# Rotated queries and keys: turned by VectorE in 32x32 squares and moved by DMA, instead of turned by TensorE

## The chip, the cores and the metric

One core of a Trainium2 chip runs the whole program. The metric is the device time of one execution in microseconds, the median of the runs. All times below are microseconds unless they say ns.

## What is computed

Two stacks of two layers each, over 256 tokens of width 1024, in float32. The change touches the first stack alone. Cut to what matters there:

```python
def hybrid_layer(x, ...):
    u = rms_norm(x) @ w_in                       # 1024 x 10240
    qa, ka, va, za, qb, kb, vb, zb, ga, gb = split_cols(u)
    qa, ka = partial_rope(qa), partial_rope(ka)  # 16 heads of 64, first 16 features rotated
    ya = dilated_mixture(qa, ka, va) * silu(za)
    qb, kb = partial_rope(qb), partial_rope(kb)
    ob = diff_attention(qb[0::2], qb[1::2], kb[0::2], kb[1::2], vb, lam)
    yb = rms_norm(ob) * (1 - lam_init) * silu(zb)
    merged = sigmoid(ga) * (ya @ w_proj_a) + sigmoid(gb) * (yb @ w_proj_b)
    return x + merged @ w_out
```

Every attention needs scores q.k for each head. TensorE contracts over partitions, so for the scores the 64 features of a head have to lie on partitions, while the projection leaves tokens on partitions.

## The kernel before

The work is a plan of *pieces*. A weight section of 1024x1024 is two jobs of 512 columns, each of four pieces of 256 rows, so a section is eight pieces. The ten sections of `w_in` come in the order qa, ka, va, za, qb, kb, vb, ga, gb, zb, then the projections pa, pb and out. Numbering the pieces of a layer from 0, qa is 0 to 7, ka 8 to 15, va 16 to 23, za 24 to 31, qb 32 to 39, kb 40 to 47, vb 48 to 55, ga 56 to 63.

SP loads a *unit* (two pieces, 1 MB) into one of four `raw` buffers (line 366), as soon as VectorE has taken the unit that was there (`lo_ready`). ScalarE rounds a piece to `hi` (line 383, ring of 6), VectorE subtracts to get `lo` (line 393, ring of 5, up to three pieces ahead), and TensorE multiplies three times per weight tile: lines 430, 431, 432 (411 and 413, or 420 to 422, where the output is wanted by features). That is twelve 512-column matmuls in a piece.

`plan_one` writes the order by hand: `p.run(jobs, between)` puts the steps of `between[i]` behind piece i of a section. All engines walk the same list of steps, each doing its own part, in order. In the steps around the change:

- `("rope", "qa", tb)`: GpSimd rotates the first 16 features of each head in place, for 128 tokens (lines 1034 to 1039).
- `("turn", "qa", f)`: TensorE transposes four 128x128 blocks into a PSUM bank (`turn_fill`, line 464), and VectorE copies the bank to `qT` or `kT` (line 843). Four of these steps turn a section.
- `("a_scores", h)`, `("b_scores", h)`: TensorE multiplies q and k of heads for attention a (lines 620 and 623, four heads at every fourth step) and for attention b (lines 665 and 666, two at every second). Two heads sit in the two halves of the partitions, and their matmuls run side by side in the array. VectorE takes the maximum with the mask (line 1006).

`buf` are nine buffers of 128x2048: q_tok, k_tok, qT, kT, va, vb, ya, yb, z.

Of the kernel before, what the change touches and what calls it, by code (L numbers as in the profile page):

```python
# [20 lines left out]
ALU = mybir.AluOpType  # L21
# [20 lines left out]
LO_LEAD = 3  # L42
LEVELS = 7
# [205 lines left out]
def plan_one(layer):  # L249

    p = Plan(layer)
    sec = lambda n, i: section(n, "w_in", i * D, 0)
    if layer == 0:
        p.steps += [("turn", "h", 0), ("turn", "h", 1), ("warm", 10)]
    late = lambda name: [("later", name)] if layer == 0 else []
    p.run(sec("qa", 0), [[("turn", "h", 2), ("stat", 0)], [("turn", "h", 3), ("stat", 1), ("rstd",)], ])
    p.run(sec("ka", 1), [[("rope", "qa", 0)], [("rope", "qa", 1)], late("lambda")] + turns("qa"))
    p.run(sec("va", 2), [[("rope", "ka", 0)], [("rope", "ka", 1)], [("half_row",)]] + turns("ka"))
    work = turned_values("a", HEADS)
    p.run(by_features(sec("za", 3)))  # L260
# [12 lines left out]
    p.run(section("out", "w_out", 0, 1), turns("mix", 2) + [[], []] + [ahead(t) for t in turns("h", 0, 2)]  # L273
          + [ahead([("final_row",), ("stat", 0)]) if layer == DEPTH - 1 else []])
    return p


class Core:


    def __init__(self, nc, ctx, ins, plans):
# [32 lines left out]
        self.first_loaded = sem("first_loaded")  # L314

# [38 lines left out]
    def load_unit(self, sp, u):  # L354

        job, n, layer = self.units[u]
        if u >= RAW:
            sp.wait_ge(self.lo_ready, 2 * (u - RAW) + 2)
        slot, k = u % RAW, job.unit
        r0 = (job.row + n * k) * P  # L360
        src = self.ins[job.weight][layer, r0:r0 + k * P, job.col:job.col + job.cols].rearrange("(k p) c -> p k c", p=P)
        dst = self.raw[slot][:, 0:k * job.cols].rearrange("p (k c) -> p k c", k=k)
        if u == 0:
            sp.dma_start(dst[:, 0:k // 2, :], src[:, 0:k // 2, :]).then_inc(self.first_loaded, 16)
            dst, src = dst[:, k // 2:, :], src[:, k // 2:, :]
        sp.dma_start(dst, src).then_inc(self.unit_loaded[slot], 16)

# [168 lines left out]
def block_one(nc, core, s, plans, ins):  # L536
# [5 lines left out]
    target = {"qa": qT, "ka": kT, "qb": qT, "kb": kT}  # L542
    xt_of = {"yb": 0, "mix": 1}
# [16 lines left out]
    parts = [(0, slice(0, P), own), (1, slice(P, 3 * P), both)]  # L560

    @core.program("tensor")
    def _(pe):
        for plan in plans:
            layer, base = plan.layer, plan.base
            turn_at = 0
            for what in plan.all_steps(s):
# [28 lines left out]
                if kind == "turn":  # L596
                    f = what[2]
                    b = (TURN, OUT)[turn_at % 2]
                    turn_at += 1
                    if arg == "h":  # L600
                        turn_input(pe, core, s, b, f)
                        continue
                    core.free(pe, b)
                    if arg in ("qa", "ka", "qb", "kb"):
                        pe.wait_ge(*at("rotated", arg))
                    elif arg == "mix":
# [5 lines left out]
                    core.hold(s, b, "cut" if arg in xt_of else "turn_copied", (arg, f))  # L612
                if kind == "a_scores" and arg % 4 == 0:
                    pe.wait_ge(*at("turn_copied", ("ka", arg // 4)))
                    for two in (arg, arg + 2):
# [42 lines left out]
                if kind == "b_scores" and arg % 2 == 0:  # L658
                    pe.wait_ge(*at("turn_copied", ("kb", arg // 2)))
                    for h in (arg, arg + 1):  # L660
                        for m in range(2):
# [3 lines left out]
                            pe.matmul(B[b][:, 0:P], qT_(qT)[r, h, 0:P], qT_(kT)[r, h, 0:P], start=True, stop=True)  # L665
                            pe.matmul(B[b][:, P:3 * P], qT_(qT)[r, h, P:S], qT_(kT)[r, h, :],  # L666
# [24 lines left out]
    def _(act):  # L691
        for plan in plans:
# [3 lines left out]
            for what in plan.all_steps(s):  # L696
# [41 lines left out]
                if kind == "evac" and arg[:2] in ("zb", "ga", "gb"):  # L738
# [4 lines left out]
                    if arg == "ga0":  # L743
                        act.wait_ge(*at("turned", ("qb", 3)))
                    if arg == "gb0":
                        act.wait_ge(*at("turned", ("kb", 3)))
# [61 lines left out]
    def _(dve):  # L808
        for plan in plans:
            layer, base = plan.layer, plan.base  # L810
            for what in plan.all_steps(s):
# [10 lines left out]
                if kind == "turn":  # L822
# [16 lines left out]
                    else:  # L839
                        dve.wait_ge(*at("turned", (arg, f)))  # L840
                        if arg in ("qb", "kb") and f == 0:
                            dve.wait_ge(*at("a_scored", HEADS - 1))
                        dve.tensor_copy(qT_(target[arg])[:, 2 * f:2 * f + 2, :], bank)\
                           .then_inc(*up("turn_copied", (arg, f)))
                if kind == "evac":
# [4 lines left out]
                    if name in ("qa", "ka", "va", "qb", "kb", "vb"):  # L850
                        if arg == "qb0":
                            dve.wait_ge(*at("turned", ("qa", 3)))
                        if arg == "kb0":
                            dve.wait_ge(*at("turned", ("ka", 3)))
# [64 lines left out]
                if kind == "a_out":  # L919
# [3 lines left out]
                    if arg == 0:  # L923
                        dve.wait_ge(*at("evac", ("za1", "gate", 1)))
                    dve.tensor_tensor(y, B[OUT][:, 0:S], qT_(z)[:, arg, :], ALU.mult).then_inc(*up("ya", arg))
# [32 lines left out]
                if kind == "b_out":  # L958
                    h = arg
                    i = (h % 2) * 2  # L960
                    dve.wait_ge(*at("b_summed", h))
                    dve.tensor_tensor(yb[:, :, h * DV:h * DV + DV],
# [23 lines left out]
    def _(sp):  # L986
        for plan in plans:
            for u in range(len(plan.units)):
                if plan.base // 2 + u >= RAW:
                    core.load_unit(sp, plan.base // 2 + u)  # L990
# [403 lines left out]
def block_two(nc, core, s, plans, ins):  # L1394
# [92 lines left out]
    def _(pe):  # L1487
        for plan in plans:
            layer, base = plan.layer, plan.base
            turn_at = 0  # L1490
            for what in plan.all_steps(s):
# [111 lines left out]
                if kind == "decay_sum":  # L1603

                    core.free(pe, TURN)
                    pe.wait_ge(*at("g"))
# [70 lines left out]
                if kind == "betas":  # L1677

                    core.free(pe, b)
                    pe.wait_ge(*at("brk"))  # L1680
# [122 lines left out]
    def _(act):  # L1803
        for plan in plans:
            layer, base = plan.layer, plan.base
            for what in plan.all_steps(s):
# [41 lines left out]
                if kind == "decay":  # L1848
                    act.wait_ge(*at("evac", "ba0"))
                    act.activation(t.beta, t.ba[:, :, 0:DHEADS], ACT.Tanh, scale=0.5).then_inc(*up("beta_tanh"))  # L1850
                    act.wait_ge(*at("abs"))
# [179 lines left out]
    def _(dve):  # L2031
        for plan in plans:
            layer, base = plan.layer, plan.base
            for what in plan.all_steps(s):
# [44 lines left out]
                if kind == "turn":  # L2079
# [39 lines left out]
                    elif arg == "v":  # L2119
                        dve.wait_ge(*at("turned", (arg, f)))  # L2120
                        dve.wait_ge(*at("beta"))
# [6 lines left out]
                    elif arg == "kd":  # L2128
                        dve.wait_ge(*at("turned", (arg, f)))
                        dve.wait_ge(*at("kds"))  # L2130
# [7 lines left out]
                if kind == "decay":  # L2138
                    y = t.ba[:, :, DHEADS:2 * DHEADS]
                    dve.wait_ge(*at("evac", "ba0"))  # L2140
                    dve.tensor_tensor(y, y, bcast(t.dtb_all[:, layer, :], 1, TB), ALU.add).then_inc(*up("y"))
                    dve.wait_ge(*at("y"))
                    dve.scalar_tensor_tensor(t.abs, y, -1.0, y, ALU.mult, ALU.max).then_inc(*up("abs"))
                    dve.wait_ge(*at("beta_tanh"))
                    dve.tensor_scalar(t.beta, t.beta, 0.5, 0.5, ALU.mult, ALU.add).then_inc(*up("beta"))
                    dve.wait_ge(*at("soft", 1))
                    dve.scalar_tensor_tensor(t.soft, y, 0.0, t.abs, ALU.max, ALU.add).then_inc(*up("softplus"))
                    dve.wait_ge(*at("softplus"))
                    dve.tensor_tensor(t.g, t.soft, bcast(t.nega_all[:, layer, :], 1, TB), ALU.mult).then_inc(*up("g"))
# [13 lines left out]
                if kind == "scales":  # L2163
                    dve.wait_ge(*at("rk"))
                    dve.wait_ge(*at("beta"))
                    dve.wait_ge(*at("ec"))
                    dve.wait_ge(*at("rotated", "sq"))
                    dve.tensor_scalar(t.future, core.upper, -1.0, -NEG, ALU.add, ALU.mult).then_inc(*up("future"))
                    dve.tensor_tensor(t.brk, t.beta, t.rk, ALU.mult).then_inc(*up("brk"))
                    dve.tensor_tensor(t.kds, t.ec[:, 1, :], t.rk[:, 0, :], ALU.mult).then_inc(*up("kds"))  # L2170
                    dve.wait_ge(*at("brk"))
                    dve.scalar_tensor_tensor(t.rs, t.ec[:, 0, :], -1.0, t.brk[:, 1, :], ALU.mult, ALU.mult)\
                       .then_inc(*up("rs"))
# [100 lines left out]
                if kind == "rows":  # L2274

                    dve.wait_ge(*at("rows", arg))
                    dve.wait_ge(*at("future"))
# [57 lines left out]
                if kind == "delta_r":  # L2335
                    dve.wait_ge(*at("from_state", arg))
                    dve.wait_ge(*at("rs"))
# [107 lines left out]
    def _(sp):  # L2445
        for plan in plans:
            for u in range(len(plan.units)):
                core.load_unit(sp, plan.base // 2 + u)
# [80 lines left out]
```

## Time and profile before

| | |
|---|---|
| median of 3 runs | 1710.27 us (1710.21 to 1710.49) |
| profiled execution, first to last instruction | 1709.1 us, TensorE's granted clock 0.999 |
| its own time as a run | not listed; the median of the runs stands 1.2 us above the span |
| TensorE, VectorE, ScalarE, GpSimd busy | 99%, 68%, 56%, 13% of the span |

Busy time counts an instruction from start to end; matmuls overlap each other, so what a matmul costs on TensorE is the distance from its start to the start of the next one. A group of rows "x4" in a timeline is four instructions merged. A float32 matmul that is no transpose appears as two MATMUL records.

### The profile page before, as it was taken

Reading aid. Unit: us, or ns where it says so; the run is one execution under the profiler, and the core shown is the slowest. Engines: PE = TensorE matmul, PEld = TensorE weight load, DVE = VectorE, ACT = ScalarE, POOL = GpSimd, SP = SyncE. Lnnn points to the kernel's source line nnn. Section 1 sums busy time; section 2 is a strip of 40 time slices with the busy share of each in tenths; the row PEclk is TensorE's granted clock in tenths of the full one; section 3 lists DMA queues with packets and bytes.
Section 4 is the critical chain, followed back from the end, with each engine's and each line's share of the span. In section 5 each row is a group of like instructions: output and inputs, shape, how many; then the busy total and the mean of one; then the engine's idle time right before and its main releaser. Section 6 shows DMA issues by size and latency. Waiting matters only on the chain.

```text
span 1709.1 us, 28116 instructions
## 1 busy us (share of the span) xinstructions
PE 1683.8 (99%) x10761; PEld 1378.8 (81%) x10761; DVE 1167.3 (68%) x2160; ACT 959.5 (56%) x1818; POOL 228.2 (13%) x318
## 2 busy tenths in 40 slices
PE   9999999999999999999999999999999999999998
PEld 7887888888878888876787878888876787778887
DVE  6666667766666676678867766656678867676665
ACT  5358475453674754578645455555677645464553
POOL 2202100022030000332202000000332203000000
PEclk9999999999999999999999999999999999999999
DMA  8443544555434345632323455555632333455552
GB/s 309 161 173 125 172 148 149 193 180 194 152 132 164 135 163 173 232 125 100 124 100 110 161 171 182 180 185 174 222 123 100 124 100 125 149 172 195 181 181 85
DMA packets 137120, 270.09 MB, mean 158 GB/s; under 512 B 5535, under 2 KB 8731, under 8 KB 136987
## 3 DMA queue, kind: packets, MB, share of 16 engines
q1 hardware_dynamic: 134928, 265.44, 45.1%
q10 hardware_dynamic: 2059, 2.85, 0.5%
q8 instruction: 87, 1.43, 0.3%
q14 instruction: 46, 0.38, 0.1%
HBM read 267.23 MB, written 1.05 MB: 157 GB/s over the span
## 4 chain that ended last, share of the span: by engine, by line
PE 85%; ACT 5%; DVE 4%; POOL 3%; issue 2%; DMA 0%; DVEq 0%; POOLq 0%; ACTq 0%; SPq 0%
PE bank L430 21%; PE bank L432 20%; PE bank L431 20%; PE bank L411 5%; PE bank L413 3%; PE bank L464 3%; PE bank L422 1%; PE bank L420 1%; PE bank L421 1%; ACT scratch L1963 1%; ACT hi L383 1%; DVE lo L393 1%; PE bank L1751 1%; DVE buf L2115 1%; PE bank L640 1%
## 5 line engine op out<-in xcount | busy, mean ns | idle before, releaser
L430 PE MATMUL bank<-hi,xhl 128*128 128x512 f32 (+1 forms) x1728 | 700.2, 405 | 3.6 <-DVE lo L393 2.1
L432 PE MATMUL bank<-hi,xhl 128*128 128x512 f32 (+1 forms) x1728 | 673.5, 390 | 0.0
L431 PE MATMUL bank<-lo,xhl 128*128 128x512 f32 (+1 forms) x1728 | 671.2, 388 | 0.0
L393 DVE TENSOR_TENSOR lo<-raw,hi 128x1024 fp32r<-128x1024 f32 (+1 forms) x504 | 613.9, 1237 | 49.5 <-PE bank L432 35.5
L383 ACT ACTIVATE hi<-raw 128x1024 fp32r<-128x1024 f32 (+1 forms) x504 | 519.4, 1050 | 213.7 <-PE bank L432 183.0
L430 PEld LDWEIGHTS bank<-hi,xhl 128*128 128x128 f32 x1728 | 324.7, 188 | 79.0 <-issue 14.5
L432 PEld LDWEIGHTS bank<-hi,xhl 128*128 128x128 f32 x1728 | 324.3, 188 | 70.8
L431 PEld LDWEIGHTS bank<-lo,xhl 128*128 128x128 f32 x1728 | 325.5, 188 | 57.2
L411 PE MATMUL bank<-xhl,hi 128*128 128x512 f32 x384 | 136.0, 398 | 0.0
L413 PE MATMUL bank<-xhl,lo 128*128 128x256 f32 x384 | 107.8, 281 | 0.0
L411 PEld LDWEIGHTS bank<-xhl,hi 128*128 128x128 f32 x384 | 72.1, 188 | 17.8
L528 POOL TENSOR_SCALAR small<-small 128x1 f32<-128x1 f32 (+1 forms) x13 | 4.7, 364 | 575.4 <-ACT scratch L521 575.2
L413 PEld LDWEIGHTS bank<-xhl,lo 128*128 128x128 f32 x384 | 72.5, 189 | 0.5
L2115 DVE SCALAR_TENSOR_TENSOR buf<-bank,small,buf 128x255 f32<-128x255 f32 (+1 forms) x144 | 62.8, 477 | 2.5
L464 PE MATMUL bank<-square,buf 128*128 128x128 f32 x408 | 61.0, 273 | 3.2 <-ACT buf L1915 1.6
L464 PEld LDWEIGHTS bank<-square,buf 128*128 128x128 f32 x408 | 48.5, 140 | 17.2 <-issue 6.8
L1034 POOL TENSOR_TENSOR scratch<-buf,rope 128x128 f32<-128x128 f32 (+1 forms) x24 | 24.6, 1025 | 282.6 <-DVE buf L859 239.0
L859 DVE TENSOR_SCALAR buf<-bank,small 128x512 f32<-128x512 f32 x48 | 33.8, 747 | 40.2 <-PE bank L432 40.2
L2243 DVE TENSOR_TENSOR buf<-bank,buf 128x256 f32<-128x256 f32 x48 | 17.0, 417 | 59.4 <-ACT buf L1948 59.4
L420 PE MATMUL bank<-xhl,hi 128*128 128x256 f32 x192 | 54.6, 285 | 0.0
L1006 DVE CUSTOM_DVE_ANT_0 scratch<-bank,masks 128x128 f32<-128x128 f32 (+1 forms) x128 | 38.8, 350 | 22.9 <-PE bank L666 18.0
L422 PE MATMUL bank<-xhl,lo 128*128 128x256 f32 x192 | 54.3, 283 | 0.0
(323 smaller groups left out, 1944.5 us busy)
## 6 DMA issues: line engine op xcount, KB each, us to landing
raw<-in_w_in SPq DMA_DIRECT2D x135, 1024.0 KB, 5.0
raw<-in_w_ff SPq DMA_DIRECT2D x64, 1024.0 KB, 5.3
raw<-in_w_proj_a SPq DMA_DIRECT2D x8, 1024.0 KB, 5.0
raw<-in_w_proj_b SPq DMA_DIRECT2D x8, 1024.0 KB, 5.0
raw<-in_w_out SPq DMA_DIRECT2D x8, 1024.0 KB, 5.2
raw<-in_w_up_sw SPq DMA_DIRECT2D x8, 1024.0 KB, 4.9
raw<-in_w_up_dn SPq DMA_DIRECT2D x8, 1024.0 KB, 4.9
raw<-in_w_o SPq DMA_DIRECT2D x8, 1024.0 KB, 4.8
```

The lines of the kernel that those rows point to most:

```text
L383: act.activation(self.hi[g % HI_RING][:, 0:w], src, ACT.Copy).then_inc(self.hi_ready, 1)
L393: dve.tensor_tensor(self.lo[g % LO_RING][:, 0:w], src, self.hi[g % HI_RING][:, 0:w].bitcast(F32), ALU.subtract).then_inc(self.lo_ready, 1)
L411: pe.matmul(out, hi, self.xhl[job.xt][:, row, :, :].rearrange("p a t -> p (a t)"), start=first, stop=False, skip_group_check=True)
L413: mm = pe.matmul(out[:, 0:S], lo, xh[:, row, :], start=False, stop=last, skip_group_check=True)
L420: pe.matmul(out, hi, xh[:, row, :], start=first, stop=False, skip_group_check=True)
L422: mm = pe.matmul(out, lo, xh[:, row, :], start=False, stop=last, skip_group_check=True)
L430: pe.matmul(out, xh[:, row, t], self.hi[slot % HI_RING][:, w], start=first, stop=False)
L431: pe.matmul(out, xh[:, row, t], self.lo[slot % LO_RING][:, w], start=False, stop=False)
L432: mm = pe.matmul(out, xl[:, row, t], self.hi[slot % HI_RING][:, w], start=False, stop=last)
L464: mm = pe.transpose(bank[:, (j * TB + tb) * P:(j * TB + tb + 1) * P], src[:, tb, c:c + P], core.ident)
L1006: ins = dve.tensor_tensor_reduce(masked[:, to], bank[:, cols], core.masks[:, which, keys], -SCALE, -NEG if negsink is None else negsink, A ...
L2115: ins_ = dve.scalar_tensor_tensor(y, x, w, y, ALU.mult, ALU.add)
```

## The change

The four sections qa, ka, qb, kb are no longer transposed by TensorE. A step `flip` takes the place of four `turn` steps:

- VectorE turns 32x32 squares (`dve.transpose`, two instructions per section, one per 128 tokens), from the rotated section into a buffer that is free then (`flip_from`). It writes 4-byte elements with a step of 16 elements.
- SP waits for that and issues 16 transfers within SBUF, each of 32 partitions by 512 contiguous elements (2 KB), which put the squares where a full transpose has them. They stand in SP's queue between the weight loads. `load_ahead` issues loads up to a fixed number of pieces ahead, so that SP can walk the steps.
- In `qT` and `kT` neighbouring tokens of a feature now lie 16 elements apart. `flipped(buf, f)` is the view that the score matmuls read, for both operands.
- The ropes of qb and kb stand one section earlier, or one or two pieces earlier. Some semaphores of the second block share a name; their order is the same.

```diff
-    p.run(sec("ka", 1), [[("rope", "qa", 0)], [("rope", "qa", 1)], late("lambda")] + turns("qa"))
-    p.run(sec("va", 2), [[("rope", "ka", 0)], [("rope", "ka", 1)], [("half_row",)]] + turns("ka"))
+    p.run(sec("ka", 1), [[("rope", "qa", 0)], [("rope", "qa", 1)], late("lambda"), [], [("flip", "qa")], [], [], []])
+    p.run(sec("va", 2), [[("rope", "ka", 0)], [("rope", "ka", 1)], [("half_row",)], [], [("flip", "ka")], [], [], []])
...
-    p.run(sec("kb", 5), work[8:16])
-    p.run(sec("vb", 6), [work[16] + [("rope", "qb", 0)], work[17] + [("rope", "qb", 1)], work[18] + [("rope", "kb", 0)], [("rope", "kb", 1)]]
-          + turns("qb"))
+    queries = [[("rope", "qb", 0)], [("rope", "qb", 1)], [], [], [], [("flip", "qb")], [], []]
+    p.run(sec("kb", 5), [a + q for a, q in zip(work[8:16], queries)])
+    p.run(sec("vb", 6), [work[16] + [("rope", "kb", 0)], work[17] + [("rope", "kb", 1)], work[18], [],
+                         [("flip", "kb")], [], [], []])
     work = difference(DHEADS)
-    p.run(sec("ga", 8), turns("kb") + work[:4])
+    p.run(sec("ga", 8), [[]] * 4 + work[:4])
...
+    def load_ahead(self, sp, g):
+
+        while self.units_issued < min(len(self.units), (g + LOAD_LEAD) // 2 + 1):
+            self.load_unit(sp, self.units_issued)
+            self.units_issued += 1
...
+    flip_from = {"qa": ya, "ka": yb, "qb": yb, "kb": ya}
+    def flipped(buf, f):
+
+        return buf[:, :, :].rearrange("p a b -> p (a b)").rearrange("p (t f b) -> p f b t", f=KB, b=TB)[:, f]
...
-                            pe.matmul(B[b][:, 0:P], qT_(qT)[r, h // 2, 0:P], qT_(kT)[r, h // 2, 0:P],
+                            pe.matmul(B[b][:, 0:P], flipped(qT, h // 2)[r, 0], flipped(kT, h // 2)[r, 0],
...
-                            pe.matmul(B[b][:, P:3 * P], qT_(qT)[r, h // 2, P:S], qT_(kT)[r, h // 2, :],
+                            pe.matmul(B[b][:, P:3 * P], flipped(qT, h // 2)[r, 1], flipped(kT, h // 2)[r],
...
+                if kind == "flip":
+
+                    dve.wait_ge(*at("rotated", arg))
...
+                    for tb in range(TB):
+                        y = flip_from[arg][:, :, :].rearrange("p a b -> p (a b)")\
+                            .rearrange("p (j a f t) -> p t j f a", j=4, f=KB, t=TB)[:, tb]
+                        ins = dve.transpose(y, source[arg][:, tb, :].rearrange("p (f j a) -> p j f a", f=KB, j=4))
+                    ins.then_inc(*up("flip_turned", arg))
...
+            for what in plan.all_steps(s):
+                kind, arg = what[0], what[1] if len(what) > 1 else None
+                if kind == "piece":
+                    core.load_ahead(sp, plan.base + arg)
+                if kind == "flip":
+                    y = flip_from[arg][:, :, :].rearrange("p a b -> p (a b)").rearrange("p (j x) -> p j x", j=4)
+                    to = target[arg][:, :, :].rearrange("p a b -> p (a b)").rearrange("p (i x) -> p i x", i=4)
+                    sp.wait_ge(*at("flip_turned", arg))
+                    if arg in ("qb", "kb"):
+                        sp.wait_ge(*at("a_scored", HEADS - 1))
+                    if arg != "qa":
+                        sp.wait_ge(*at("flipped", ({"ka": "qa", "qb": "ka", "kb": "qb"}[arg], 3, 3)))
+                    for i in range(4):
+                        for j in range(4):
+                            sp.dma_start(to[QUARTER * j:QUARTER * (j + 1), i, :], y[QUARTER * i:QUARTER * (i + 1), j, :])\
+                              .then_inc(*up("flipped", (arg, i, j), 16))
```

On TensorE, in section ka of layer 0, before:

```order
L432 MATMUL bank<-hi,xhl 128x512
L464 MATMUL bank<-square,buf 128x128 x4
L430 MATMUL bank<-hi,xhl 128x512
L431 MATMUL bank<-lo,xhl 128x512
L432 MATMUL bank<-hi,xhl 128x512
```

and now, at the same place:

```order
L441 MATMUL bank<-hi,xhl 128x512
L439 MATMUL bank<-hi,xhl 128x512
L440 MATMUL bank<-lo,xhl 128x512
L441 MATMUL bank<-hi,xhl 128x512
L439 MATMUL bank<-hi,xhl 128x512
```

The four transposes between the pieces are gone; the big matmuls around them are the same (line 430 is now 439).

On VectorE, in sections ka and va, before (line 859 takes a section's half out of PSUM):

```order
L393 TENSOR_TENSOR lo<-raw,hi 128x1024
L859 TENSOR_SCALAR buf<-bank,small 128x512 x2
L843 COPY buf<-bank 128x512
L393 TENSOR_TENSOR lo<-raw,hi 128x1024
L843 COPY buf<-bank 128x512
L393 TENSOR_TENSOR lo<-raw,hi 128x1024
L843 COPY buf<-bank 128x512
L393 TENSOR_TENSOR lo<-raw,hi 128x1024
L843 COPY buf<-bank 128x512
```

and now:

```order
L402 TENSOR_TENSOR lo<-raw,hi 128x1024
L877 TENSOR_SCALAR buf<-bank,small 128x512 x2
L402 TENSOR_TENSOR lo<-raw,hi 128x1024
L865 STREAM_TRANSPOSE buf<-buf 128x4x8x32 x2
L402 TENSOR_TENSOR lo<-raw,hi 128x1024 x3
L877 TENSOR_SCALAR buf<-bank,small 128x512 x2
```

Four copies, each between two pieces, became two turns behind each other.

On SP, the whole first layer's loads stood in one run:

```order
L1082 DMA narrow<-in_narrow 128x448
L366 DMA raw<-in_w_in 128x4x512 x36
L366 DMA raw<-in_w_proj_a 128x4x512 x4
L366 DMA raw<-in_w_proj_b 128x4x512 x4
```

and now have the transfers between them:

```order
L369 DMA raw<-in_w_in 128x4x512 x8
L1023 DMA buf<-buf 32x512 x16
L369 DMA raw<-in_w_in 128x4x512 x4
L1023 DMA buf<-buf 32x512 x16
L369 DMA raw<-in_w_in 128x4x512 x13
L1023 DMA buf<-buf 32x512 x16
L369 DMA raw<-in_w_in 128x4x512 x3
L1023 DMA buf<-buf 32x512 x16
```

Sixteen small transfers per section moved in front of every later load.

## Rows read from the trace of the kernel before

**Rows 1.** The page: busy time, share of the span, instructions of each engine.

```profile
PE 1683.8 (99%) x10761; PEld 1378.8 (81%) x10761; DVE 1167.3 (68%) x2160; ACT 959.5 (56%) x1818; POOL 228.2 (13%) x318
```

**Rows 2.** The page: the chain that ended last, share by engine.

```profile
PE 85%; ACT 5%; DVE 4%; POOL 3%; issue 2%; DMA 0%; DVEq 0%; POOLq 0%; ACTq 0%; SPq 0%
```

**Rows 3.** The page's groups: busy us, mean ns | idle us before, releaser.

```profile
L430 PE MATMUL bank<-hi,xhl 128*128 128x512 f32 (+1 forms) x1728 | 700.2, 405 | 3.6 <-DVE lo L393 2.1
```

**Rows 4.** Timeline of TensorE, sections with transposes: start, duration, instruction.

```profile
72.29 0.60 PE L464 MATMUL bank<-square,buf 128*128 128x128 f32 x4
72.64 0.48 PE L430 MATMUL bank<-hi,xhl 128*128 128x512 f32 x1
72.96 0.39 PE L431 MATMUL bank<-lo,xhl 128*128 128x512 f32 x1
...
75.48 0.60 PE L464 MATMUL bank<-square,buf 128*128 128x128 f32 x4
75.84 0.48 PE L430 MATMUL bank<-hi,xhl 128*128 128x512 f32 x1
```

**Rows 5.** Timeline of TensorE, twelve big matmuls and nothing between.

```profile
62.04 0.39 PE L430 MATMUL bank<-hi,xhl 128*128 128x512 f32 x1
...
64.76 0.39 PE L430 MATMUL bank<-hi,xhl 128*128 128x512 f32 x1
```

**Rows 6.** Groups of VectorE, shapes apart: the copies of line 843.

```profile
L843 DVE COPY buf<-bank 128x512 f32<-128x512 f32 x32 | 22.1, 690 | 29.1 <-PE bank L464 29.1
```

**Rows 7.** Timeline of TensorE at the first scores of attention a.

```profile
107.44 0.39 PE L432 MATMUL bank<-hi,xhl 128*128 128x512 f32 x1
107.76 0.49 PE L620 MATMUL bank<-buf 64*128 64x128 f32 x4
108.08 0.60 PE L623 MATMUL bank<-buf 64*128 64x256 f32 x4
108.52 0.39 PE L620 MATMUL bank<-buf 64*128 64x128 f32 x4
108.74 0.60 PE L623 MATMUL bank<-buf 64*128 64x256 f32 x4
109.27 0.50 PE L430 MATMUL bank<-hi,xhl 128*128 128x512 f32 x1
```

**Rows 8.** Groups of VectorE, shapes apart; one line of a source view (ns min/median/max).

```profile
L897 DVE TENSOR_TENSOR buf<-buf 128x1024 f32<-128x1024 f32 x4 | 4.9, 1225 | 0.1
L918 DVE RECIPROCAL small<-small 128x2 f32<-128x2 f32 x32 | 5.0, 156 | 0.7 <-ACT scratch L758 0.7
L2162 DVE COPY small<-bank x4: 165/172/175, 805.3 to 1348.0; 128x16 f32<-128x16 f32 x4
```

**Rows 9.** Windows: busy of PE, PEld, DVE, ACT, POOL; clock, DMA share, GB/s.

```profile
34.00:56.00 22.00, 22.00 (x106) 18.13 (x106) 16.77 (x28) 8.38 (x9) 8.69 (x10) 1.00 0.46 155
134.00:166.00 32.00, 32.00 (x187) 24.28 (x186) 21.19 (x60) 25.50 (x69) 7.04 (x10) 1.00 0.39 132
```

**Rows 10.** Timelines of VectorE, SP, ScalarE and TensorE: the load of piece 32.

```profile
71.20 1.22 DVE L393 TENSOR_TENSOR lo<-raw,hi 128x1024 fp32r<-128x1024 f32 x1
...
77.97 0.37 SPq L366 DMA_DIRECT2D raw<-in_w_in  x1
...
95.53 2.94 ACT L383 ACTIVATE hi<-raw 128x1024 fp32r<-128x1024 f32 x3
...
96.27 4.63 DVE L393 TENSOR_TENSOR lo<-raw,hi 128x1024 fp32r<-128x1024 f32 x4
...
104.92 0.40 PE L430 MATMUL bank<-hi,xhl 128*128 128x512 f32 x1
```

**Rows 11.** Loads: SP's issue (ns), KB and us to landing, SP's waits.

```profile
L366 SPq DMA_DIRECT2D raw<-in_w_in x140: 367/368/1147, 2.1 to 1379.0; - x140
...
raw<-in_w_in SPq DMA_DIRECT2D x135, 1024.0 KB, 5.0
...
buf<-in_positions ACTq DMA_DIRECT2D x2, 0.5 KB, 2.1
...
SPq L366 <- DVE lo L393: 1560.1, 247, 13.4
```

More of the change, by code:

```diff
@@ L42 @@
 LO_LEAD = 3
+LOAD_LEAD = 11
 LEVELS = 7
@@ L314, in __init__ @@
         self.first_loaded = sem("first_loaded")
+        self.units_issued = RAW
     def hold(self, s, bank, name, key=0):
@@ L611, in _ @@
                     core.turn_bank[s.stage, arg, f] = b
-                    core.hold(s, b, "cut" if arg in xt_of else "turn_copied", (arg, f))
+                    core.hold(s, b, "cut", (arg, f))
                 if kind == "a_scores" and arg % 4 == 0:
-                    pe.wait_ge(*at("turn_copied", ("ka", arg // 4)))
+                    if arg == 0:
+                        pe.wait_ge(*at("flipped", ("qa", 3, 3)))
+                        pe.wait_ge(*at("flipped", ("ka", 3, 3)))
                     for two in (arg, arg + 2):
@@ L658, in _ @@
                 if kind == "b_scores" and arg % 2 == 0:
-                    pe.wait_ge(*at("turn_copied", ("kb", arg // 2)))
+                    if arg == 0:
+                        pe.wait_ge(*at("flipped", ("qb", 3, 3)))
+                        pe.wait_ge(*at("flipped", ("kb", 3, 3)))
                     for h in (arg, arg + 1):
@@ L664, in _ @@
                             r = slice(HD * m, HD * m + HD)
-                            pe.matmul(B[b][:, 0:P], qT_(qT)[r, h, 0:P], qT_(kT)[r, h, 0:P], start=True, stop=True)
-                            pe.matmul(B[b][:, P:3 * P], qT_(qT)[r, h, P:S], qT_(kT)[r, h, :],
+                            pe.matmul(B[b][:, 0:P], flipped(qT, h)[r, 0], flipped(kT, h)[r, 0], start=True, stop=True)
+                            pe.matmul(B[b][:, P:3 * P], flipped(qT, h)[r, 1], flipped(kT, h)[r],
                                       start=True, stop=True).then_inc(*up("b_scored", (h, m)))
@@ L743, in _ @@
                     if arg == "ga0":
-                        act.wait_ge(*at("turned", ("qb", 3)))
+                        act.wait_ge(*at("flip_turned", "qb"))
                     if arg == "gb0":
-                        act.wait_ge(*at("turned", ("kb", 3)))
+                        act.wait_ge(*at("flip_turned", "kb"))
                     for tb in range(TB):
@@ L838, in _ @@
                         ins.then_inc(*up("cut", (arg, f)))
[L839 to L844, printed above, removed]
+                if kind == "flip":
+                    dve.wait_ge(*at("rotated", arg))
+                    if arg == "qb":
+                        dve.wait_ge(*at("flipped", ("ka", 3, 3)))
+                    if arg == "kb":
+                        dve.wait_ge(*at("cut", ("ya", HEADS // 2 - 1)))
+                    for tb in range(TB):
[3 more added lines that the diff above has]
+                    ins.then_inc(*up("flip_turned", arg))
                 if kind == "evac":
@@ L961, in _ @@
                     dve.wait_ge(*at("b_summed", h))
+                    if h == 0:
+                        dve.wait_ge(*at("flipped", ("qb", 3, 3)))
                     dve.tensor_tensor(yb[:, :, h * DV:h * DV + DV],
@@ L2164, in _ @@
                     dve.wait_ge(*at("rk"))
-                    dve.wait_ge(*at("beta"))
+                    dve.wait_ge(*at("gates", "beta"))
                     dve.wait_ge(*at("ec"))
                     dve.wait_ge(*at("rotated", "sq"))
[L2168 to L2171, printed above, removed]
+                    dve.tensor_scalar(t.future, core.upper, -1.0, -NEG, ALU.add, ALU.mult).then_inc(*up("scales", "future"))
+                    dve.tensor_tensor(t.brk, t.beta, t.rk, ALU.mult).then_inc(*up("scales", "brk"))
+                    dve.tensor_tensor(t.kds, t.ec[:, 1, :], t.rk[:, 0, :], ALU.mult).then_inc(*up("scales", "kds"))
+                    dve.wait_ge(*at("scales", "brk"))
                     dve.scalar_tensor_tensor(t.rs, t.ec[:, 0, :], -1.0, t.brk[:, 1, :], ALU.mult, ALU.mult)\
-                       .then_inc(*up("rs"))
+                       .then_inc(*up("scales", "rs"))
                 if kind == "f_cut":
@@ L2445, in _ @@
     def _(sp):
-        for plan in plans:
-            for u in range(len(plan.units)):
-                core.load_unit(sp, plan.base // 2 + u)
+        for u in range(core.units_issued, len(core.units)):
+            core.load_unit(sp, u)
 def build(nc, ins, out, tally=None):
```

40 lines of the change are left out of this document (16 added, 24 removed).

## The prediction

> **What bounds the kernel now.** I read the busy shares first: TensorE is busy in 99% of a span of 1709.1 us, VectorE in 68%, ScalarE in 56% [rows 1]. The chain that ended last lies on TensorE for 85%, with ScalarE 5% and VectorE 4% [rows 2]. The costliest group, the first of the three multiplications of a weight tile, has 3.6 us of idle time before it over 1728 instructions, most of it on VectorE's lo [rows 3]. So TensorE is the bound and its own instructions are its time: what leaves its stream is gained, what lengthens one is paid, and the other engines matter only when they come late.
>
> **Transposes removed.** Four sections (qa, ka, qb, kb), four groups each, two layers: 32 groups of four 128x128 transposes. The timeline shows two groups [rows 4]: with one in between, the two big matmuls around it would start 0.23 apart; the group starts at 72.29, the next big matmul at 72.64, and the one behind that only at 72.96. Start to start, 72.64 to 75.84 is one piece of twelve big matmuls with one group: 3.20 us. A piece without a group takes 2.72 us, 62.04 to 64.76 [rows 5]. The difference is 0.48 us. Reading only around the group gives the lower value: 72.29 to 72.96 is 0.67, less one matmul of 0.23, is 0.44; the rest is that the following matmuls start 0.230 instead of 0.227 apart, which need not vanish. So 32 groups are worth 14.1 to 15.4 us. I take 0.47 each: **-15.0 us**.
>
> **Copies removed, squares added on VectorE.** 32 copies of 0.69 us leave, and with them 29.1 us in which VectorE waited for the transposes [rows 6]. In come 16 turns of 128x1024 (two a section). The trace has no such instruction. Lower bound: nothing moves 1024 elements on VectorE in less than the 1.23 us of an SBUF to SBUF operation [rows 8]; so 2.4 us a section against 2.8 removed. Upper bound: three times that row, 3.7 us each, 7.4 us a section, because the results are written with a step of 64 bytes. I take 2 us each. The cover is the lo lead: in 34 to 56 us (section ka) VectorE is busy 16.8 of 22 us, in 134 to 166 us 21.2 of 32 [rows 9]. By my values section ka becomes 16.8 - 2.1 + 4.0 = 18.7 of some 20.5 us. Even 7.4 us are 22 us once; the lead absorbs it (the VectorE row at 96.27 is pieces 31 to 34, so 32 is done at 98.6, and TensorE wants it at 104.92 [rows 10], some 6 us). Cost 0. Without that cover it would be the excess over the lead, in each of eight places.
>
> The Trainium skill, "Vector Engine (DVE) Microarchitecture Reference", section 5.2, gives 2.5 ns a column where the destination steps by 24 words; by that each turn would take an estimated 2.6 us. No row here shows it, and the sum stays as it is.
>
> **Sixteen transfers on SP.** They stand in the same queue as the weight loads. Each issue of a load holds SP for 0.368 us, so 16 hold it 5.9 us [rows 11]; SP has idle time for it, 1560 us of waiting for lo. What is late next is the load behind them. Take ka in layer 0: VectorE is through with lo about 72.4 and turns until 76.4; SP issues until 82.3; the load that went out at 77.97 [rows 10] goes out 4.4 us later. One section moves 1 MB, as much as one load, which lands in 5.0 us [rows 11]; behind it the load lands at 82.3 + 5 + 5 = 92.3. ScalarE wants it at 95.53 and TensorE wants the piece at 104.92 [rows 10]. Bounds for the transfers: 5 us at a load's rate, and 16 times the 2.1 us in which the smallest transfer lands, 34 us, if they ran one by one. I take 5, since a load is itself many rows in flight. Cost 0. The consumers are far: qa and ka are turned in the pieces 12 and 20 and first read at 107.76 [rows 7]; kb is turned after piece 52 and first read after piece 60, eight pieces or 22 us later. So the waits on the landed squares cost nothing either. The three waits of SP (turned, the previous section landed, the last a-score) end before or with the turning; only loads queue behind them.
>
> **Ropes and buffers.** The ropes of qb and kb move one section and one or two pieces ahead; GpSimd is busy 228 us of the span [rows 1]. The renamed semaphores of the second block add no wait. Cost 0.
>
> **Scores read with a step.** This is the disputed term. Both operands of every score matmul now step by 16 elements, 64 bytes. Before, a pair of heads takes 0.22 us for its 128-column and 0.44 us for its 256-column matmuls (108.52 to 108.74, 108.08 to 108.52 [rows 7]), 0.66 us. There are 16 pairs a layer, 8 of attention a and 8 of attention b: 32 pairs, 21 us on the bound engine. The trace has no stepped TensorE operand. What it shows: the fp32r stream of the weights takes 512 columns in 0.227 us, 0.44 ns a column [rows 5]; the fp32 scores take 256 columns in 0.44 us for four instructions in two row groups, 0.85 ns a column and pass. So the same port delivers contiguous words twice as fast as the scores ask. Lower bound of the added cost: 0 (a gain is excluded, nothing is shortened). Upper bound: a stepped word costs a VectorE column, 1.20 ns (1.225 us for 1024 [rows 8]): factor 1.4, +8.6 us. A wider one: every column takes twice its present time, +21 us. The only stepped read in the trace is VectorE's copy of 16 columns out of PSUM, 172 ns, against 156 for two unstepped ones [rows 8], which says little but shows no cliff. I take 0, since the port has a factor of two to spare, and keep +21 for the range.
>
> The Trainium skill speaks against this change here: "Advanced Engine Details and Errata", section "SBUF Cachelines", has 16-byte lines of which at least two hits each are needed for full speed, with a penalty when each access meets another line; at 64 bytes every one does. By my rows' rate, the change is then a question of how large the penalty is: up to a factor of two on the port hides in the fp32 rate, beyond it the scores stretch.
>
> **Sum.** -15.0 + 0 + 0 + 0 = -15.0 against the median: the profiled span of 1709.1 us becomes 1694.1, and with the 1.2 us by which the median stands above the span, **1695.3 us**.
>
> **Rivals.**
> *The stepped reads lengthen the scores* (the other side). If a stepped column takes a second time its present slot, +21.1 - 15.0 = +6.1: 1716.4 us; if three times, +42 - 15 = +27: 1737 us. It decides from the point where the score streams take 1.7 times as long (15.0 of 21.1). For it: every word is in another line, and it hits both operands; the weight loads, 128 stepped columns each, may become the longer side. Against it: the factor of two of the port. A smaller form (1.1 to 1.6 times) leaves 2 to 13 us of gain, 1697 to 1708 us. The skill's line rule is this rival's mechanism.
> *The transfers starve the weight ring.* If the 16 run one by one, a section holds the queue 34 us; a load then comes 34 less the 12 us between its arrival and TensorE's need, some 20 us, too late, eight times: beyond 1800 us. With half the overlap, 15 us a section, a few us in all: 1700 us. For it: one queue, 32 descriptors each; against it: a load of 1 MB that lands in 5.0 us has its rows in flight together, and the distance above.
> *VectorE becomes late.* If a turn takes over 5.5 us, section ka needs 14.7 + 11 = 26 us in 20.5 and the lead is spent; about 3 us in each of four places, 1707 us. Against it: four times the nearest row.
> *The change does not do what it says*: TensorE would have to idle where the transposes stood. With 3.6 us of idle time in the group [rows 3] and leads of 6 us that is excluded but for a few tenths.
>
> **Chances.** Forecast (gain 13 to 16 us) 0.46; scores a little longer or some waits (gain over 3.4 us) 0.11; gains and costs cancel 0.06; scores stretched beyond 1.85 times 0.28; loads starved 0.05; VectorE late 0.04, of which half still gains. 0.2% is 3.4 us, about what a measurement of this kernel can tell from no change. Faster 0.58, same 0.06, slower 0.36. The range must reach into the doubled scores: 1692.5 (0.56 us a group) to 1722 (2.3 times); the rest, with tripled scores and starved loads, is some 0.15 to 0.2. The forecast's own range is 1693 to 1698.
>
> **What would show it.** Right: no L464 transposes in these sections; pieces of 2.72 us there; score matmuls of a pair still 0.66 us apart and their durations (272 and 377 ns) unchanged; turns near 2 us; loads still landing within 5 to 12 us; L430's idle time unchanged. Wrong: score matmuls whose starts lie 0.4 us and 0.9 us apart, or longer weight loads between them; idle time of TensorE before L439 released by lo; ScalarE waiting for a DMA. The stepped read is what would make the prediction wrong.

## The result, and the profile after

The change made the kernel slower: 1717.21 us median (1716.99 to 1717.47, 5 runs) against 1710.27 us (1710.09 to 1710.69, 5 runs), ratio 1.004 with a 95% interval of 1.0028 to 1.0051. The forecast was 1695.3 us, so the time lies 22 us away from it, and within a microsecond of the first rival, "a stepped column takes a second time its present slot", 1716.4 us. It lies inside the wide range and on the other side of no change than the one forecast.

The page of the changed kernel, its busy shares and the group of the first big matmul, beside [rows 1, 3]:

```profile
span 1715.3 us, 27940 instructions
PE 1690.1 (99%) x10633; PEld 1380.4 (80%) x10633; DVE 1175.0 (68%) x2144; ACT 959.5 (56%) x1818; POOL 225.8 (13%) x318
L439 PE MATMUL bank<-hi,xhl 128*128 128x512 f32 (+1 forms) x1728 | 696.9, 403 | 3.6 <-DVE lo L402 2.1
```

TensorE has 128 instructions fewer, is busy 6.3 us longer, and has not waited any longer: 25.2 us of the span lie outside its busy time, 25.3 before, and the 3.6 us of idle time of the first group and their releaser are those of before. So the time did not go into a wait. It is in TensorE's own instructions.

The same piece of section ka, after (start, duration, instruction; twelve big matmuls from the first row to the second), and the first scores of attention a, beside [rows 5, 7]:

```profile
49.36 0.39 PE L439 MATMUL bank<-hi,xhl 128*128 128x512 f32 x1
...
52.08 0.39 PE L439 MATMUL bank<-hi,xhl 128*128 128x512 f32 x1
...
103.03 0.39 PE L441 MATMUL bank<-hi,xhl 128*128 128x512 f32 x1
103.34 0.80 PE L634 MATMUL bank<-buf 64*128 64x128 f32 x4
103.96 1.05 PE L637 MATMUL bank<-buf 64*128 64x256 f32 x4
104.82 0.62 PE L634 MATMUL bank<-buf 64*128 64x128 f32 x4
105.26 1.04 PE L637 MATMUL bank<-buf 64*128 64x256 f32 x4
106.24 0.50 PE L439 MATMUL bank<-hi,xhl 128*128 128x512 f32 x1
```

The piece without transposes takes 2.72 us, as forecast. The group of four heads takes 3.21 us from the start of the big matmul ahead of it to that behind it (103.03 to 106.24), where it took 1.83 us (107.44 to 109.27 in [rows 7]): 1.38 us more. The matmuls of 256 columns start 0.86 us before the next group instead of 0.44, and the 128-column ones 0.44 before theirs instead of 0.22: the distances of 0.9 and 0.4 us that the prediction had named as its sign of being wrong. The source views of the two lines say the same for all 64 records of each (ns min/median/max). The 256-column line before:

```profile
L623 PEld LDWEIGHTS bank<-buf x64: 188/188/188, 108.0 to 491.3; 64*128 64x128 f32 x64
L623 PE MATMUL bank<-buf x64: 376/377/378, 108.1 to 491.5; 64*128 64x256 f32 x64
```

and both lines after:

```profile
L634 PEld LDWEIGHTS bank<-buf x64: 288/295/307, 103.3 to 495.0; 64*128 64x128 f32 x64
L634 PE MATMUL bank<-buf x64: 390/390/575, 103.3 to 495.2; 64*128 64x128 f32 x64
...
L637 PEld LDWEIGHTS bank<-buf x64: 289/298/307, 103.8 to 495.4; 64*128 64x128 f32 x64
L637 PE MATMUL bank<-buf x64: 603/603/609, 104.0 to 495.8; 64*128 64x256 f32 x64
```

Each section, from the start of its first big matmul to that of the next section, layer 0, in us (worked out from the starts in the three traces; the last column is the best version, told below):

```
section   before   after   small_rows
ka         23.69   21.76     21.76
va         23.93   21.99     21.99
qb         29.24   32.00     29.23
kb         31.97   34.73     31.97
vb         26.45   24.66     24.66
ga         26.65   25.99     24.59
gb         29.75   32.61     29.76
zb         27.95   29.36     27.96
```

The other sections differ by less than 0.1 us, and layer 1 repeats the table. The gain is there, in ka, va, vb and ga, 7.7 us a layer. The loss is in the four sections that hold scores: qb, kb and gb have two groups each (+2.8), zb one (+1.4), and ga one of its own, which leaves 0.66 of its 2.06 us of gain. Together the five are 11.2 us a layer (eight groups of 1.38 us are 11.0). For both layers: -15.4 + 22.4, some 7 us. The first big matmul of this execution starts 0.6 us earlier than in that of the kernel before, and the span grew by 6.2.

What VectorE, SP and ScalarE did at section va of layer 0, in the timelines:

```profile
69.25 3.81 DVE L865 STREAM_TRANSPOSE buf<-buf 128x1024 f32<-128x1024 f32 x2
...
73.09 10.58 SPq L1023 DMA_DIRECT2D buf<-buf  x16
83.71 1.71 SPq L369 DMA_DIRECT2D raw<-in_w_in  x3
...
91.12 2.94 ACT L392 ACTIVATE hi<-raw 128x1024 fp32r<-128x1024 f32 x3
```

And over the program, the turns and the issues of the transfers in the source views:

```profile
L865 DVE STREAM_TRANSPOSE buf<-buf x16: 1937/1978/2018, 47.3 to 524.9; 128x1024 f32<-128x1024 f32 x16
...
L1023 SPq DMA_DIRECT2D buf<-buf x128: 507/591/1457, 51.1 to 537.2; - x128
```

The list of DMA issues gives the median from issue to landing in its last column:

```profile
buf<-buf SPq DMA_DIRECT2D x128, 64.0 KB, 2.0
```

A turn took 1.98 us. An issue of a transfer took 0.59 us in the median, not a load's 0.368; with the gaps between them the sixteen held SP for 10.6 us here instead of the forecast 5.9, and three loads queued up behind. The transfers landed 2.0 us after their issue (median), longer than one issue takes, so they overlapped. The loads had enough lead: ScalarE split the same pieces at 91.12, 9.4 us before section qb began at 100.50, the same lead as before the change (95.53 for a start at 104.92 [rows 10]). TensorE did not wait.

### The profile page after: what moved, and what is told of

Its sections match the earlier page's. It is cut to its first block, busy times and chain, and to the rows that moved or that the text cites. A ratio compares the mean times of both kernels' runs of the same rounds, so it can differ in the third digit from the quotient of the medians.

```text
span 1715.3 us, 27940 instructions
## 1 busy us (share of the span) xinstructions
PE 1690.1 (99%) x10633; PEld 1380.4 (80%) x10633; DVE 1175.0 (68%) x2144; ACT 959.5 (56%) x1818; POOL 225.8 (13%) x318
## 4 chain that ended last, share of the span: by engine, by line
PE 85%; ACT 5%; DVE 4%; POOL 3%; issue 2%; DMA 0%; DVEq 0%; POOLq 0%; ACTq 0%; SPq 0%
PE bank L439 21%; PE bank L441 20%; PE bank L440 20%; PE bank L420 5%; PE bank L422 3%; PE bank L473 2%; PE bank L431 1%; PE bank L430 1%; PE bank L429 1%; ACT scratch L1997 1%; ACT hi L392 1%; DVE lo L402 1%; PE bank L1785 1%; PE bank L637 1%; PE bank L682 1%
## 5 line engine op out<-in xcount | busy, mean ns | idle before, releaser
L429 PE MATMUL bank<-xhl,hi 128*128 128x256 f32 x192 | 54.6, 284 | 0.0
L430 PE MATMUL bank<-xhl,hi 128*128 128x256 f32 x192 | 54.3, 283 | 0.0
L1982 ACT ACTIVATE buf<-bank 128x256 f32<-128x256 f32 x48 | 14.5, 390 | 56.0 <-PE bank L422 56.0
```

Source lines behind the costliest of these rows:

```text
L429: pe.matmul(out, hi, xh[:, row, :], start=first, stop=False, skip_group_check=True)
L430: pe.matmul(out, hi, xl[:, row, :], start=False, stop=False, skip_group_check=True)
```

## The experiments

The theory after the result: the step of 64 bytes in the score operands costs the whole 22 us, and nothing else of the change costs anything. Within it, two operands are stepped, so either the moving stream (theory M) or the weight loads (theory W) carries the price, or both (B). The rival: the time comes from the moved ropes, the transfers or the turns.

**moving_step.** Only the keys, the moving operand, are read with the step. The queries' columns are then the wrong ones, so the scores are of other numbers.

```diff
-    pe.matmul(B[b][:, 0:P], flipped(qT, h // 2)[r, 0], flipped(kT, h // 2)[r, 0],
+    pe.matmul(B[b][:, 0:P], qT_(qT)[r, h // 2, 0:P], flipped(kT, h // 2)[r, 0],
```

(and likewise in the three other score matmuls)

> The changed kernel, but the stationary operand of every score matmul is read in contiguous words, so that only the moving operand (the keys) steps by 16 elements; the queries' columns are then the wrong ones, the work is the same in number and size. Theory M (the stepped moving stream is what costs): as the changed kernel, 1717 us, a pair of heads at 1.3 us. Theory W (the stepped weight loads cost): 1695 us, a pair at 0.66 us, weight loads back at 188 ns. Theory B (both count, each about half): 1706 us.

Measured: 1714.72 us, ratio to before 1.0025 (1.0015 to 1.0035).

**weights_step.** Only the queries, the stationary operand, are read with the step; the keys' columns are the wrong ones.

```diff
-    pe.matmul(B[b][:, 0:P], flipped(qT, h // 2)[r, 0], flipped(kT, h // 2)[r, 0],
+    pe.matmul(B[b][:, 0:P], flipped(qT, h // 2)[r, 0], qT_(kT)[r, h // 2, 0:P],
```

> The changed kernel, but the moving operand (the keys) is read in contiguous words, and only the stationary operand (the queries) steps by 16 elements; the keys' columns are then the wrong ones. Theory M: 1695 us, matmul durations back at 272 and 377 ns although the weight loads still take about 295. Theory W: 1717 us. Theory B: 1706 us.

Measured: 1704.60 us, ratio 0.9966 (0.9952 to 0.9979). The source views of line 637, first moving_step:

```profile
L637 PEld LDWEIGHTS bank<-buf x64: 202/203/203, 103.8 to 493.7; 64*128 64x128 f32 x64
L637 PE MATMUL bank<-buf x64: 603/604/606, 104.0 to 494.2; 64*128 64x256 f32 x64
```

then weights_step:

```profile
L637 PEld LDWEIGHTS bank<-buf x64: 307/309/313, 103.7 to 486.1; 64*128 64x128 f32 x64
L637 PE MATMUL bank<-buf x64: 379/434/487, 103.8 to 486.3; 64*128 64x256 f32 x64
```

Neither M nor W holds alone, and B's even split doesn't either. Against the 1695.5 us of the version without any step (below), the moving step costs 19.2 us and the stationary step 9.1, and both together 21.7 (19.5, 9.4 and 22.2 if each is taken against the kernel before that ran beside it). They do not add up, and the traces fit this reading: the longer weight load of the next matmul is done while the stretched stream of the present one runs, and shows where the stream is short. In weights_step the record behind a 128-column one starts 0.22 us after it (103.63 and 103.85 in the trace), as far apart as the weight loads, although that stream needs only 0.11 us without a step. In the changed kernel it starts 0.22 us after it too (103.74 and 103.96), but there the stretched stream itself takes as long. In both kernels the rest of the change (turns, transfers, moved ropes) is in place, and weights_step is faster than before.

**before_stepped.** The kernel before, with the transposes and copies as they were, and both operands read with the step (other numbers, the same amount). The two waits for the turned keys are for the fourth copy.

```diff
-                    pe.wait_ge(*at("turn_copied", ("ka", arg // 4)))
+                    pe.wait_ge(*at("turn_copied", ("ka", 3)))
...
-    pe.matmul(B[b][:, 0:P], qT_(qT)[r, h // 2, 0:P], qT_(kT)[r, h // 2, 0:P],
+    pe.matmul(B[b][:, 0:P], flipped(qT, h // 2)[r, 0], flipped(kT, h // 2)[r, 0],
```

> The kernel before, with its 32 groups of transposes, but both operands of the scores read with the step of 16 elements (columns in the wrong order). If the step is the whole cost of the change, 1710.3 + 22 = 1732 us, and the difference to the changed kernel is the transposes' 15 us. If the added time of the changed kernel comes from the moved ropes, the transfers or the turns on VectorE, 1710 us.

Measured: 1732.81 us, ratio 1.013 (1.0116 to 1.0144), 22.3 us over the kernel before. So the step alone, with nothing else of the change, costs what the change lost, and the rival falls. In its trace the sections qb, kb and gb take 32.00, 34.73 and 32.62 us, within 0.01 of the changed kernel. From here to the changed kernel are 15.6 us, the transposes.

**keys_in_runs.** The first repair. The queries, the stationary operand, stay at their one step. For the keys, the moving operand, VectorE writes each square's 32 tokens side by side, and the matmul reads four runs of 32 for each 128 tokens.

```diff
+    def in_runs(buf, f):
+        return buf[:, :, :].rearrange("p a b -> p (a b)").rearrange("p (i f b a) -> p f b i a", i=4, f=KB, b=TB)[:, f]
...
-                            .rearrange("p (j a f t) -> p t j f a", j=4, f=KB, t=TB)[:, tb]
+                            .rearrange("p (j a f t) -> p t j f a" if arg[0] == "q" else "p (j f t a) -> p t j f a",
+                                       j=4, f=KB, t=TB)[:, tb]
```

> The changed kernel with another order of the keys alone: VectorE writes each turned square of the keys as 32 neighbouring elements, the 16 transfers stay 2 KB a row, and the moving operand reads four runs of 32 elements 512 apart. The queries (stationary) keep the step of 16. Full computation. Theory M: 1695 us, faster than both kernels. Theory W: 1717 us. The turns of the keys, written without a step, take about 1.2 us instead of 1.98 if the step costs VectorE too.

Measured: 1704.77 us, ratio 0.9965 (0.9951 to 0.9979): the computation whole, and faster than both kernels. It is the time of weights_step, so runs of 32 are as good as contiguous. The expectation of theory M was 9.8 us too low; the queries' weight loads account for it, since the next version, without their step, takes 9.3 us less. The turns of this kernel:

```profile
L870 DVE STREAM_TRANSPOSE buf<-buf x16: 1201/1590/2005, 47.7 to 515.0; 128x1024 f32<-128x1024 f32 x16
```

Half of them, the keys', write without a step and take 1.2 us; the queries' still take 2.0.

**small_rows.** keys_in_runs, and the queries' transfers put each run of 32 elements (128 bytes) in its place, so that the stationary operand is contiguous. VectorE writes the queries' squares side by side too, so no turn has a step any more, and the score matmuls read the queries through `qT_`, as before the change; the lines below show only the transfers.

```diff
-                            sp.dma_start(to[QUARTER * j:QUARTER * (j + 1), i, :], y[QUARTER * i:QUARTER * (i + 1), j, :])\
-                              .then_inc(*up("flipped", (arg, i, j), 16))
+                            dst, src = to[QUARTER * j:QUARTER * (j + 1), i, :], y[QUARTER * i:QUARTER * (i + 1), j, :]
+                            if arg[0] == "q":
+                                dst = target[arg][QUARTER * j:QUARTER * (j + 1), :, :].rearrange("p a b -> p (a b)")\
+                                    .rearrange("p (k i a) -> p i k a", i=4, a=QUARTER)[:, i]
+                                src = src.rearrange("p (k a) -> p k a", a=QUARTER)
+                            sp.dma_start(dst, src).then_inc(*up("flipped", (arg, i, j), 16))
```

> keys_in_runs, and the queries are put in place by the same 16 transfers a section, but in rows of 128 bytes (512 rows per transfer instead of 32), so that the stationary operand is contiguous too and no score operand has a step. Full computation. If steps are the only cost: the transposes' 15.5 us are gained whole, 1694.8 us, and a pair of heads is back at 0.66 us. If 16 times as many rows are no longer hidden: sections ka or va (after qa) and vb (after qb) grow over 21.8 and 24.7 us, or ScalarE waits for the weight loads; with some 15 us lost in each of four places as much as 1750 us.

Measured: 1695.50 us (1695.24 to 1695.66), against 1710.73 before on the same chip, ratio 0.9911 (0.9897 to 0.9924). This is the best version. Its source views:

```profile
L869 DVE STREAM_TRANSPOSE buf<-buf x16: 1202/1220/1241, 47.8 to 508.0; 128x1024 f32<-128x1024 f32 x16
...
L1032 SPq DMA_DIRECT2D buf<-buf x128: 557/620/2298, 50.1 to 519.5; - x128
...
DMA to landing us min/median/max: 2.0/2.1/5.1
...
L641 PEld LDWEIGHTS bank<-buf x64: 188/188/188, 104.1 to 479.7; 64*128 64x128 f32 x64
L641 PE MATMUL bank<-buf x64: 376/377/378, 104.2 to 479.9; 64*128 64x256 f32 x64
```

The scores are back at 377 and 188 ns. The queries' transfers have sixteen times as many rows. Taken apart, one of their issues takes 0.63 us in the median against 0.59 for the keys' 2 KB rows, and the landing 2.1 us against 2.0. For the queries the 2 KB rows, which brought the step with them, saved nothing. For the keys they did not need the step: the keys still move in 2 KB rows here and are read in runs of 32.

**keys_only.** Only ka and kb take the new way, in runs of 32; qa and qb are transposed by TensorE as before.

```diff
-    p.run(sec("ka", 1), [[("rope", "qa", 0)], [("rope", "qa", 1)], late("lambda"), [], [("flip", "qa")], [], [], []])
+    p.run(sec("ka", 1), [[("rope", "qa", 0)], [("rope", "qa", 1)], late("lambda")] + turns("qa"))
...
-    queries = [[("rope", "qb", 0)], [("rope", "qb", 1)], [], [], [], [("flip", "qb")], [], []]
+    queries = [[("rope", "qb", 0)], [("rope", "qb", 1)], [], [], [], [], [], []]
...
-                         [("flip", "kb")], [], [], []])
+                         [("turn", "qb", 0), ("flip", "kb")]] + turns("qb", 1))
```

> Only the keys go through VectorE and the transfers, and are read in runs of 32; the queries are transposed by TensorE as before and stay contiguous. Full computation. Half the transposes leave: -7.7 us, and nothing is added to the scores: 1702.6 us, slightly under keys_in_runs (-15.5 + 9.8 for the stepped weight loads = 1704.8).

Measured: 1703.40 us against 1710.73, ratio 0.9958 (0.9944 to 0.9971), -7.3 us, 0.8 us short of the expectation. Half the transposes are worth about half of the 15.2 us.

**step_table.** How does the price depend on the step? Here attention a reads the moving operand, and attention b the stationary one, with a different step for each pair of heads (other numbers are multiplied; amount and order are the same).

```diff
+    steps = ((1, 2, 3, 4, 6, 8, 12, 16), (1, 1, 1, 5, 7, 9, 10, 14))
...
-    pe.matmul(B[b][:, 0:P], flipped(qT, h // 2)[r, 0], flipped(kT, h // 2)[r, 0],
+    pe.matmul(B[b][:, 0:P], qT_(qT)[r, h // 2, 0:P], moving(kT, h // 2, layer, True)[r],
...
-    pe.matmul(B[b][:, 0:P], flipped(qT, h)[r, 0], flipped(kT, h)[r, 0], start=True, stop=True)
+    pe.matmul(B[b][:, 0:P], weights(qT, h, layer)[r], qT_(kT)[r, h, 0:P], start=True, stop=True)
```

> The changed kernel, with other columns read by the scores, so that it computes something else: attention a reads the moving operand with steps 1, 2, 3, 4, 6, 8, 12, 16 elements (heads 0-1, 2-3, ...) in the first layer and in pairs, fours, eights of neighbours 16 apart, then steps 5, 7, 9, 10, 14 in the second; attention b reads the stationary operand with steps 1, 2, 3, 4, 6, 8, 12, 16 and 1, 1, 1, 5, 7, 9, 10, 14. If the price comes with every change of a 16-byte line, a column costs 0.85 ns up to step 2 or 3 and 1.68 ns from step 4; if it depends on banks, it varies among the larger steps. Runs of two or more should be free if one fetch serves two words.

Measured: 1706.74 us, a single run; what counts are its rows. Line 656, the 256-column records of one pair of heads each, by window: moving step 2, then 3, 4, 8, 16, and last pairs of neighbours 16 apart:

```profile
L656 PE MATMUL bank<-buf x4: 382/383/384, 104.7 to 104.9; 64*128 64x256 f32 x4
...
L656 PE MATMUL bank<-buf x4: 506/507/507, 118.8 to 119.1; 64*128 64x256 f32 x4
...
L656 PE MATMUL bank<-buf x4: 626/626/627, 119.9 to 120.3; 64*128 64x256 f32 x4
...
L656 PE MATMUL bank<-buf x4: 636/636/637, 137.3 to 137.7; 64*128 64x256 f32 x4
...
L656 PE MATMUL bank<-buf x4: 603/604/604, 154.6 to 155.1; 64*128 64x256 f32 x4
...
L656 PE MATMUL bank<-buf x4: 374/375/377, 438.2 to 438.5; 64*128 64x256 f32 x4
```

Line 701, the weight loads of one pair each: stationary step 2, 3, 4, 8, 12:

```profile
L701 PEld LDWEIGHTS bank<-buf x4: 192/193/193, 205.1 to 205.3; 64*128 64x128 f32 x4
...
L701 PEld LDWEIGHTS bank<-buf x4: 257/257/257, 218.7 to 218.9; 64*128 64x128 f32 x4
...
L701 PEld LDWEIGHTS bank<-buf x4: 326/326/326, 219.6 to 220.0; 64*128 64x128 f32 x4
...
L701 PEld LDWEIGHTS bank<-buf x4: 331/332/334, 235.2 to 235.6; 64*128 64x128 f32 x4
...
L701 PEld LDWEIGHTS bank<-buf x4: 366/366/366, 250.0 to 250.3; 64*128 64x128 f32 x4
```

From start to start of the records of one row group, the 64 partitions of one head (227, 341 and 451 ns for 256 columns at steps 2, 3 and 4), the moving stream needs 0.89 ns a column at step 2, 1.33 at step 3, 1.76 at 4, and 1.68 to 1.80 at the nine larger steps tried, 5 to 16. Pairs, fours and eights of neighbours 16 apart need 0.86, the contiguous rate. The price grows up to step 4 and is then nearly flat; the expectation of two levels alone missed step 3, which lies between them.

That is close to what lines of 16 bytes, four elements, would give: a column touches 1/2, 3/4 and 1 line at steps 2, 3 and 4, and 0.89, 1.33 and 1.76 ns are all 1.76 to 1.78 ns a line. The fit is not exact. Pairs 16 apart touch half a line a column too and take 0.86, not 0.89, and step 16 takes 1.68. The weight loads rise in the same way up to step 4, but step 12, with 366 ns, is dearer than 8 (332) and 16 (309), which lines don't explain.

## Why the prediction was wrong, step by step

- **Transposes removed**, -15.0 us: right. The sections lost 15.4, before_stepped to the changed kernel is 15.6, and small_rows against before 15.2. small_rows, which has no step, takes 1695.5 us, the time that the sum had forecast (1695.3). The higher of the two readings (0.48 us a group, a whole piece with and without) was the better one: the slightly slower matmuls behind a group went with it.
- **VectorE**, cost 0 at 2 us a turn: right; 1.98 us measured. The upper bound of three times the nearest row was not needed. The estimate of 2.6 us, from the Trainium skill's 2.5 ns a column, is above the row: 1978/1024 is 1.93 ns for the step of 16 elements, 1.19 without. Its figure is for a step of 24 words, which no run here has.
- **SP and the transfers**, cost 0: right in the sum, mis-sized in a term. An issue took 0.59 us and not 0.368, some ten microseconds a section on SP instead of 5.9. What I took as 5 us of transfer came out hidden in the issues, since each landed 2.0 us after its own.
- **Ropes, buffers, semaphores**, cost 0: right; every section without scores or transposes kept its time.
- **Scores read with a step**, taken as 0: this is the step that failed, and the only one that moved the total. It cost 21.7 us in the changed kernel, where I had kept 21 for the range; the moving operand's stretched stream alone costs 19.2. The prediction said "the same port delivers contiguous words twice as fast as the scores ask", which its rows bear out (0.44 against 0.85 ns a column), and drew from it that a stepped read has a factor of two to spare, which does not follow. If the unit is a line of 16 bytes, the fast contiguous stream takes four words from each: 0.44 ns a column is 1.77 ns a line, in the very rows I had [rows 5]. A column at step 16 wants a whole line in 0.85 ns. The right use of those rows was 1.77/0.85 = 2.1 times the stream, near the price of the first rival (twice); the step table gives 1.68/0.85 = 2.0. The upper bound "a stepped word costs a VectorE column", 1.4 times, was too low as well: nothing tied the one engine's rate to the other's fetches.
- **Chances**: the stated 0.58 for faster and 0.36 for slower are 0.59 and 0.35 when their parts are added up, which changes nothing.

The Trainium skill had said it: "Advanced Engine Details and Errata", section "SBUF Cachelines", with lines of 16 bytes and at least two hits on each for full speed. The step table's moving streams agree (step 2, two hits a line, is nearly free at 0.89 ns; pairs 16 apart are free at 0.86; from step 4 on, one hit a line, 1.68 to 1.80). I had weighed this rule and let a rate argument outvote it with 0.46 against 0.28, without asking in which unit the port counts. The weight loads, which I had named only as a possible longer side, went the same way, from 188 to some 300 ns.

The first rival had the mechanism, the place and the price (1716.4 us). The rivals on the transfers and on VectorE did not come about: TensorE's idle time in the first group is what it was, and a load landed after 5.1 us in the median, before 5.0.

## What to carry to other kernels

Work out an access price in the unit that the memory delivers. A rate measured on contiguous words does not say how fast stepped ones come; if several words come with one fetch, divide the rate by their number before spending it on a stepped read. When a layout has to have a step somewhere, put it where it is hidden: here TensorE is the bound, and the DMA rows of 128 bytes that avoid the queries' step cost nothing measurable, while that step cost 9 us on TensorE. First look whether the step is needed at all: the keys lost theirs by another order of VectorE's writes and a read in runs. And where only one operand can't be read in runs, the step was cheaper on the stationary side, 9.1 us against 19.2.

## What the runs showed of the hardware

- TensorE's fp32 moving operand, 64 partitions, two heads side by side: 0.86 ns a column contiguous, in pairs, fours and eights of neighbours 16 elements apart, and in runs of 32; 0.89, 1.33, 1.76 ns at steps 2, 3, 4; 1.68 to 1.80 at steps 5 to 16 (step_table). Within this band step 16 was cheapest and 8 dearest, which the line alone does not explain; that stays open.
- Stationary operand of 64x128 fp32: the load takes 188 ns, at steps 2, 3, 4, 8, 12 it takes 193, 257, 326, 332, 366 ns, at 16 about 309 (step_table). Why 12 is dearest stays open.
- A 128x1024 turn on VectorE takes 1.22 us with contiguous runs of 32 at its destination (small_rows) and 1.98 us at a step of 16 (the changed kernel).
- An SP issue of a transfer within SBUF of 32 partitions by 2 KB took 0.59 us, and 0.63 us with the same bytes in rows of 128 bytes (small_rows); that of a 128-partition load took 0.37 us.
